# One sum moved to GpSimd at the entry of the attention layer, with the order of four engines rewritten around it

## The reference, cut to what matters

```
def sqrelu_mlp(h, w_up, w_down):
    return jnp.square(jax.nn.relu(h @ w_up)) @ w_down

for i in range(DEPTH):
    h = rmsnorm(x, g_mix_pre[i])
    m = conformer_conv(h, ...) if i % 2 == 0 else forgetting_attention(h, w_in, b_f, w_o)
    x = x + rmsnorm(m, g_mix_post[i])
    h = rmsnorm(x, g_ffn_pre[i])
    x = x + rmsnorm(sqrelu_mlp(h, w_up[i], w_down[i]), g_ffn_post[i])
```

## Time and profile before

| | |
|---|---|
| median of 3 runs | 1134.79 us (1134.19 to 1137.14) |
| the profiled execution, its own time | 1137.0 us |
| its span in the trace | 1135.3 us |
| PE busy | 1114.7 us (98%) |
| DVE busy | 933.9 us (82%) |
| ACT busy | 766.4 us (68%) |
| POOL busy | 292.0 us (26%) |

### The profile page before, as it was taken

One profiled execution on the slowest core, in us unless ns is written; L12 is line 12 of the kernel. 1 busy time (PEld: TensorE's weight loads), 2 busy tenths in 40 slices (PEclk: granted clock), 3 DMA queues, 4 the chain that ended last, 5 costly groups with the idle time before them and its releaser, 6 DMA issues. The chain is left out here.

```text
span 1135.3 us, 18229 instructions
## 1 busy us (share of the span) xinstructions
PE 1114.7 (98%) x6452; PEld 976.9 (86%) x6452; DVE 933.9 (82%) x1348; ACT 766.4 (68%) x1266; POOL 292.0 (26%) x269
## 2 busy tenths in 40 slices
PE   8999999999999999999999999999999999999997
PEld 7788888987898998998887888878888998988986
DVE  5899965679889689688798888894789889688688
ACT  6778878556785584675787777775566783674764
POOL 5688870221111020112421111100312020111014
PEclk9999989999999999999999999999999999999999
DMA  5322132275966676595222423232477777567673
GB/s 165 103 74 74 38 110 57 60 226 146 196 163 134 195 162 162 130 234 112 57 56 68 104 65 87 84 84 74 145 204 159 180 168 183 120 143 193 160 196 100
DMA packets 137268, 146.73 MB, mean 129 GB/s; under 512 B 5949, under 2 KB 108349, under 8 KB 136682
## 3 DMA queue, kind: packets, MB, share of 16 engines
q1 hardware_dynamic: 112300, 109.68, 30.8%
q0 software_dynamic: 24816, 35.92, 19.8%
q10 hardware_dynamic: 78, 0.16, 0.1%
HBM read 137.09 MB, written 6.29 MB: 126 GB/s over the span
## 5 line engine op out<-in xcount | busy, mean ns | idle before, releaser
L1542 ACT ACTIVATE whi<-mraw 128x1024 fp32r<-128x1024 f32 x212 | 221.5, 1056 | 149.1 <-PE psum L1236 94.5
L2218 DVE TENSOR_TENSOR wlo<-mraw,whi 128x1024 fp32r<-128x1024 f32 x212 | 256.9, 1223 | 68.5 <-ACT whi L1542 68.1
L1234 PE MATMUL psum<-whi,aop_hi 128*128 128x512 f32 x448 | 176.3, 394 | 1.4 <-ACT acc L1843 0.9
L1235 PE MATMUL psum<-wlo,aop_hi 128*128 128x512 f32 x448 | 174.6, 390 | 0.0
L1236 PE MATMUL psum<-whi,aop_lo 128*128 128x512 f32 x448 | 174.6, 390 | 0.0
L887 PE MATMUL psum<-hhi,whi 128*128 128x512 f32 x372 | 149.3, 401 | 0.8 <-DVE wlo L2207 0.5
L889 PE MATMUL psum<-hhi,wlo 128*128 128x512 f32 x372 | 145.5, 391 | 0.0
L888 PE MATMUL psum<-hlo,whi 128*128 128x512 f32 x372 | 145.3, 391 | 0.0
L1222 PE MATMUL psum<-hhi,wlo 128*128 128x256 f32 x384 | 108.8, 283 | 0.0
L1221 PE MATMUL psum<-xlo,whi 128*128 128x256 f32 x384 | 108.8, 283 | 0.0
L1220 PE MATMUL psum<-hhi,whi 128*128 128x256 f32 x384 | 108.7, 283 | 0.0
(11 more groups left out here) (320 smaller groups left out, 2839.8 us busy)
## 6 DMA issues: line engine op xcount, KB each, us to landing
mraw<-in_mlp_w_up SPq DMA_DIRECT2D x64, 512.0 KB, 7.0
mraw<-in_mlp_w_down SPq DMA_DIRECT2D x64, 512.0 KB, 5.3
mraw<-in_mlp_w_down POOLq DMA_DIRECT2D x40, 512.0 KB, 7.2
mraw<-in_mlp_w_up POOLq DMA_DIRECT2D x24, 512.0 KB, 7.5
wraw<-in_conv_pw_w SPq DMA_DIRECT2D x20, 512.0 KB, 4.5
wraw<-in_attn_w_in SPq DMA_DIRECT2D x16, 512.0 KB, 4.8
x_copy<-xT SPq DMA_DIRECT2D x2, 2048.0 KB, 7.4
xT<-x_copy SPq DMA_DIRECT2D x2, 2048.0 KB, 11.3
```

The costliest lines, as they stand in the source:

```text
L1234: pe.matmul(o, ah, wh, start=kt == 0 and (not kept or c == 0), stop=False)
L1235: pe.matmul(o, ah, wl, start=False, stop=False)
L1542: a.activation(split_unit(whi, e), raw_unit(l, c, e_), ACT.Copy).then_inc(s["m_hi"], 1)
L2218: d.tensor_tensor(split_unit(wlo, e), raw_unit(l, c, e_), split_unit(whi, e).bitcast(F32), ALU.subtract).then_inc(s["m_ready"], 1)
```

## The change

- The sum of slots 4 and 3 goes to slot 4 instead of slot 3, in both layers; `OUT_ACC` names slot 4 for that quarter. What it writes is no longer what the adding transfer (or `last_22`) reads.
- In layer 0 GpSimd makes this sum, with a 128x1024 add issued right behind the adding transfer. In layer 1 DVE still makes it, without the wait on `last_22`.
- GpSimd adds the first half's squares after its three small constants, no longer before them.
- PE turns blocks 0 to 3 of the first half one matmul triple earlier (n = 12 instead of 13), and blocks 4 and 5 at n = 14 instead of 15. Then each kb has gate, unit 0 and unit 1 together; unit 2's blocks 0 to 4 stand before kb = 6, its blocks 5 to 7 after kb = 7, and the second half's first two turnings follow kb = 6 and kb = 7.
- ACT makes the high part of unit 1 before the first `half_hi`, that of unit 2 after the first square, and the second half's sums of squares and root stand among `half_hi` 4 to 7; the squares 6 and 7 come after the second half's `by_token`.
- DVE splits unit 1's weights before `half_lo` 0, adds P4 at k = 3 and 4, splits unit 2's weights at k = 6, and inverts the second half's root before `half_lo` 7.

```
-OUT_ACC = ((3, 2), (1, 0))
+OUT_ACC = ((4, 2), (1, 0))
...
             g.dma_start(acc[:, ACC[P5], :, :], acc[:, ACC[P7], :, :],
                         accum_op=ALU.add).then_inc(v7_sum[0], 16)
-            add_half_squares(0)
+            g.tensor_tensor(flat(acc[:, ACC[P6], :, :]), flat(acc[:, ACC[P6], :, :]), flat(acc[:, ACC[P7], :, :]),
+                            ALU.add).then_inc(s["q_sum"], 1)
             pool.wait_ge(s["m_unit"], MLP_UNITS)
...
+            add_half_squares(0)
             add_half_squares(1)
...
-                if n == 13:
+                if n == 12:
...
-                if n == 15:
+                if n == 14:
...
-            pe.wait_ge(s["p_evac"], 5 * (CHUNKS - 1) + EVAC_NTH[P6])
-            for kb in range(2):
+            pe.wait_ge(s["p_evac"], 5 * CHUNKS)
+            for kb in range(KB):
+                if kb == 2:
+                    turned(0, 3)
+                if kb == 6:
+                    pe.wait_ge(w_ready[1], 2 * N_ATT + 2)
+                    for k in range(5):
+                        half_unit(2, 0, k)
                 pe.wait_ge(s["h1_ready"], kb + 1)
                 half_gate(0, kb)
-            pe.wait_ge(s["p_evac"], 5 * CHUNKS)
-            weights(N_ATT, 1)
-            for kb in range(KB):
-                if kb == 1:
-                    turned(0, 3)
-                if kb >= 2:
-                    pe.wait_ge(s["h1_ready"], kb + 1)
-                    half_gate(0, kb)
                 for u in range(2):
+                    if kb == 0:
+                        weights(N_ATT, u)
                     half_unit(u, 0, kb)
-            pe.wait_ge(w_ready[1], 2 * N_ATT + 2)
-            for kb in range(KB):
-                if kb == 4:
+                if kb >= 6:
                     pe.wait_ge(s["nrm_d"], 4)
-                    turned(1, 0)
-                    turned(1, 1)
+                    turned(1, kb - 6)
+            for kb in range(5, KB):
                 half_unit(2, 0, kb)
...
+            split_hi_att(1)
+            half_hi(0, 0)
+            half_hi(0, 1)
+            half_square(0, 0)
+            split_hi_att(2)
+            half_square(0, 1)
+            half_hi(0, 2)
+            half_square(0, 2)
+            half_hi(0, 3)
+            sum_squares(0, 0, 1)
+            half_hi(0, 4)
+            sum_squares(0, 1, 1)
+            half_square(0, 3)
...
             def last_21(l):
-                if l == 0:
-                    dve.wait_ge(v7_sum[0], 16 * (v_nth(0, CHUNKS - 1, "down") + 1))
-                else:
-                    dve.wait_ge(s["t22_done"], 1)
-                d.tensor_tensor(accs(P7), accs(P6), accs(P7), ALU.add).then_inc(s["q_sum"], 1)
+                dve.wait_ge(s["p_evac"], 5 * CHUNKS * (l + 1))
+                d.tensor_tensor(accs(P6), accs(P6), accs(P7), ALU.add).then_inc(s["q_sum"], 1)
...
             for k in range(KB + 1):
                 if k < KB:
                     x_half(0, k)
+                if k == 1:
+                    split_lo(N_ATT, 1)
+                if k == KB:
+                    token_inverse(0, 0)
                 if k:
                     half_lo(0, k - 1)
-                if k == 2:
-                    split_lo(N_ATT, 1)
+                if k in (3, 4):
+                    last_t2(0, k - 3)
                 if k == 6:
-                    last_21(0)
-            for tt in range(2):
-                last_t2(0, tt)
-            split_lo(N_ATT, 2, single=True)
-            token_total(0, 0)
-            token_inverse(0, 0)
+                    split_lo(N_ATT, 2, single=True)
+                    token_total(0, 0)
```

More of the change, by code:

```diff
@@ L2071, in _ @@
                 by_token(t, 1)
-            for k in range(KB):
-                half_hi(0, k)
-                if k == 1:
-                    split_hi_att(1)
-                if k:
-                    half_square(0, k - 1)
-                if k in (4, 5):
-                    sum_squares(0, k - 4, 1)
-                if k == 5:
-                    split_hi_att(2)
-            half_square(0, KB - 1)
-            for t in (0, 1):
-                sum_squares(0, t, 0)
+            split_hi_att(1)
[11 more added lines that the diff above has]
+            half_square(0, 3)
+            half_hi(0, 5)
+            sum_squares(0, 0, 0)
+            half_hi(0, 6)
+            sum_squares(0, 1, 0)
+            half_square(0, 4)
             token_root(0, 0)
+            half_hi(0, 7)
+            half_square(0, 5)
             act.wait_ge(s["tneg_done"], 2)
@@ L2088, in _ @@
                 by_token(t, 1)
+            for k in (6, 7):
+                half_square(0, k)
             for k in range(KB):
@@ L2882, in last_t2 @@
                 dve.wait_ge(s["q_sum"], 3 * l + 3)
-                o = acc[:, ACC[P7], tt, :]
+                o = acc[:, ACC[P6], tt, :]
                 d.tensor_tensor(o, o, psum[:, PBANK[P4] + tt, :], ALU.add).then_inc(s["comb"], 1)
```

## The result

The changed kernel takes 1139.45 us in the median of 19 runs, the kernel before 1135.41 us in 19 runs on the same chip. The ratio is 1.0028, with a 95% interval of 1.002 to 1.0037: slower by 3.2 us (0.0028 times 1135.4), where 0.6 us less was forecast. On the forecast's base this is 1134.79 times 1.0028 = 1138.0 us, above the range of 1132.5 to 1136.3. The profiled execution took 1138.41 us by its own time, its span is 1136.7 us, the mean granted clock of PE 0.995.

What follows compares the result with a forecast made beforehand. PE, busy 98% of the span, was taken to bound the kernel. The second half starting 0.52 us earlier plus 0.11 us at the end gave 0.63 us off 1134.79: 1134.2 us, range 1132.5 to 1136.3.

Steps and rivals of the forecast that it cites:

- the old stalls: First half: PE waits for DVE's low parts of units 1 and 2, 0.93 and 0.98 us, 1.91 us together.
- Steps 1 and 2: Entry: nothing changes up to unit 0's split; the earlier turning waits for nothing; alone, unit 1's split causes no PE stall.
- Steps 3 and 4: Entry: GpSimd's sum, ready 534.6, runs 535.94 to 538.34, delaying unit 1's split; PE stalls 1.39 us before the first gate matmul.
- The second rival: Entry: GpSimd's sum gets in ahead of unit 0's split, at 534.85; 0.2 us slower, 1135.0 us; chance 0.12.
- The second stall and its cover: At unit 2: its earlier split removes PE's 0.98 us stall, with about 0.8 us of cover.
- Port by the whole instruction: DVE and GpSimd share ports, locked for a whole instruction; DVE instructions with two SBUF inputs take part.
- Slot 3 read twice: Entry: the adding transfer reads slot 3 while GpSimd's sum does; costs nothing, or 1.6 us.
- the third rival: Entry: GpSimd's sum takes L812's whole 4.00 us, delaying unit 1's split; 1.0 us slower, 1135.8 us; chance 0.10.
- the fourth: After the entry: a later wait grows by what the entry gains; 1134.8 us; chance 0.12.
- The first rival: Entry: nothing holds up unit 1's split; both stalls go, 2.0 us gained, 1132.8 us; chance 0.16.
- The end of the program: Layer 1: DVE's sum no longer waits for `last_22` and starts 0.11 us earlier, all seen in the span.
- Given back downstream: First pair of heads or a weight transfer: a wait grows by the entry's gain; 1134.8 us; chance 0.12.

Runs made afterwards that it cites:

- Experiment 1: Changed kernel with the sum of slots 4 and 3 back on DVE in layer 0, at k = 3; ratio 1.0014 to the kernel before.
- Experiment 3: Changed kernel with GpSimd's sum waiting until DVE has scaled its two quarters; ratio 0.9993 to the kernel before.
- experiment 10: Changed kernel with PE's turnings one triple later again (n = 13 and 15); ratio 1.0003 to the kernel before.
- experiment 8: Changed kernel with 12 spare matmuls on PE in front of the first turning; ratio 1.0015 to the kernel before.
- experiment 5: Kernel of Experiment 1 with DVE's sum moved ahead of `half_lo` 2; ratio 0.9986 to the kernel before.
- experiment 6: Changed kernel, sum on DVE behind `half_lo` 2, P4 added at k = 4 and 5, ACT's `half_hi` 2 and 3 earlier; ratio 0.9988 to the kernel before.
- experiment 4: Changed kernel with GpSimd's sum cut into four adds of 128x256; ratio 1.0036 to the kernel before.
- experiment 7: Changed kernel with 24 spare matmuls on PE in front of the first turning; ratio 1.0028 to the kernel before.
- experiment 9: Changed kernel with GpSimd's sum waiting only for DVE's 128x2 negation; ratio 1.0022 to the kernel before.
- experiment 2: Kernel before with only the sum of slots 4 and 3 moved to GpSimd, old order kept; ratio 1.001 to the kernel before.

## Why the prediction was wrong

*What bounds the kernel, and the old stalls.* Right. Both stalls for weight blocks are gone. PE is busy 98% of the span in both. Without stalls the first half takes 14.28 less 1.19 = 13.09 us, forecast 13.34.

*Steps 1 and 2.* Their first sentence, "Up to unit 0's split nothing changes", is what fell. Experiment 1 shows that without GpSimd's sum they hold: turning at 1.69 us, first gate matmul at 5.08, 0.10 from where it stood, no stall ahead of it.

*Steps 3 and 4, the step that failed.* "The sum can begin at about 534.6" took the end of the transfer's recorded issue for the time from which GpSimd goes on, and "GpSimd gets its turn when unit 0's split is over" followed from it. The sum's record starts 0.62 us behind the issue's start, in the clock of before at 534.22. In the kernel before the negation stands there (533.94 to 534.20) and the scaling behind it. In the changed kernel the negation's record is open from 532.94 on, and it ends only behind GpSimd's sum; the scaling on DVE, the one on ACT, the turning and PE wait with it, 2.48 us where the prediction had no wait. The kernel before had a row that would have told it, GpSimd's next issue starting before the end of the one in front:

```profile
909.81 1.28 POOL L748 DMA_DIRECT2D mraw<-in_mlp_w_up  x1 [16.32 <-DVE wlo L2218]
910.57 1.76 POOL L756 DMA_DIRECT2D mraw<-in_mlp_w_down  x1
```

Experiment 3 shows it from the other side. There the sum comes behind the scaling, at 534.98 in the clock of before (step 3 had 534.6), and waits for unit 0's split. Its end, unit 1's split, PE's stall and the second half's start then come out within 0.2 us of step 4, and the ratio is the forecast's (0.9993; forecast 1134.2 over 1134.79 = 0.9995).

*The second rival* was the right mechanism: GpSimd in front. It was priced at +0.2 us instead of 3.2, for three reasons that the runs separate. It put GpSimd behind the scaling that PE's turning needs, while the sum caught the negation, so that the wait fell on PE inside the down product and not on a split with cover behind it. The change moved the turning one triple earlier, to where PE arrives at 1.69 us: nothing to wait for in the forecast, but 0.66 us more of standing (2.48 against 1.82, experiment 10). And it left out what a standing PE costs afterwards: 1.63 us at half clock (experiment 8; the sum above), and 1.19 us at blocks 3 and 4, where ACT's list, and by it DVE's, is tied to the last down matmul (next paragraph). The clock's part goes when the turning goes back (experiment 10) or PE is kept busy (experiment 8); the standing itself, 1.82 us and 0.87 us in experiment 10, goes only when GpSimd's sum does not stand ahead of the scaling (experiments 1, 3, 5 and 6).

*The second stall and its cover.* Right that it goes. "What would make all of this wrong is a PE stall at block 2 or at unit 2": it came at blocks 3 and 4. The prediction had "`half_hi` 2 ... ends at 540.1 + 0.40 + 0.49 = 541.0" and "PE wants block 2 ... at 542.5", a cover of 1.5 us. But 1.39 of it was the stall that PE was to have ahead of the first gate matmul, behind the same last down matmul that ACT waits for. Where PE does not stand there, the cover is not there either: the changed kernel and experiments 4, 7, 8 and 9 have 1.19 or 1.20 us at blocks 3 and 4. Where it does stand, the stalls nearly go: 0.34 us behind 0.87 in experiment 10, 0.29 behind 1.24 in experiment 3. The half clock is not the cause, since experiment 8 has none. Part may come from the P4 additions that DVE now makes between the low parts, and from ACT's high part of block 2 behind unit 2's split; experiment 6 relaxes both and has 0.37 us and less at each block. The size goes with PE's standing over all these runs, but none was made to separate the causes. I cost this at nothing; it is 1.19 us.

*Port by the whole instruction.* Right in kind. The Trainium skill, "SBUF — State Buffer", the part on the two sides of the memory, says that of the two engines the one that starts first gets the pair of ports for its whole instruction, and that VectorE's two-port modes, which a tensor_scalar can enter, take part as well as instructions with two SBUF inputs. I had read it for two-input instructions alone. The holding up of a 128x2 TENSOR_SCALAR for 2.98 us and of the scaling in experiment 9 agrees with the second half. With the first half the records do not agree as they stand: the negation's begins 0.28 us before GpSimd's (532.94 and 533.22), in experiment 4 0.29 before, and yet it is DVE that waits. Either GpSimd holds the ports earlier than its record begins or DVE later; no run tells these apart.

*Slot 3 read twice.* The sum took 2.67 us while the transfer read the same slot, 0.27 more than the subtraction of the same size in the earlier trace rows; whether the double reading or the other operation makes the 0.27, no run tells. The prediction names two rivals wrongly here: the 1.6 us for it are the third rival's size, not the fourth's, and the case in which the sum costs DVE nothing is the first, not the second. The first rival ("nothing holds up the split") and the third (a sum that runs its whole 4.00 us) did not come about: experiment 3's sum took 3.30 us, some 0.9 of it waiting for unit 0's split.

*The end of the program.* The 0.1 us is there from one sum to the next (1.64 instead of 1.74), but "The whole 0.11 us should be seen" was wrong: DVE's last addition waits for PE's last down matmul, and nothing of it is left in the span. It is worth 0.

*Given back downstream.* The kind of wait was right, its size and place only in part. The loss at the second half (+3.24) is still there at the scores (+3.57), so nothing is given back in the first pair of heads. But 1.2 us of it are gone at the end, 0.75 of them where ACT waited for a weight transfer. Of the 0.3 us at 807 us I have only that PE stood 0.15 us for a low part there in the kernel before and does not in the changed one. What also stays open is the 0.33 between second half and scores. In all kernels with the sum on GpSimd PE stands 1.11 or 1.12 us in front of the first scores, in the kernel before and in experiments 1, 5 and 6 it is 0.76 or 0.77. DVE's `gates_q` waits 0.5 instead of 0.2 us there, for ACT by the profile. The same kernels are those in which DVE has one instruction less (1347 against 1348), so the sum on GpSimd and the shorter list cannot be told apart. No run changed that place, and I have no cause for it.

## What to carry to other kernels

Before an instruction goes to GpSimd, find every DVE instruction that can meet it, tiny ones and those of one SBUF input included, and ask who waits for each: a negation of 256 numbers can pay for a whole 128x1024 add. Give the add an order against the critical short chain, by a semaphore (experiment 3: 4 us) or by leaving it on DVE in a gap that the trace shows (experiment 5), and do not cut it into pieces and hope. Price a stall of PE with what follows it, the matmuls at half clock and the engines whose lists are tied to PE's last matmul, and do not move a turning earlier where what it waits for is not early too. When a wait has cover, look whether the cover is itself a stall that the forecast counts on: it goes when the stall goes.

## What the runs showed of the hardware

- **GpSimd goes on before the recorded end of a transfer's issue.** The next instruction started 0.62 us after the start of an issue of 0.90 us in the changed kernel and in experiments 2 and 4, and 0.69 us after one of 0.98 us in experiment 9, where it waits for the negation.
- **Who gets the ports.** GpSimd got in between two back-to-back TENSOR_SCALAR of DVE (0.88 us became 3.26), and by the reading of L812's 4.00 us in the earlier trace rows did not between back-to-back differences of two SBUF operands. In experiment 3, where a split had begun 0.18 us before the sum, the sum took 3.30 us and ended 2.26 us behind the split's recorded end. DVE did not get in between four back-to-back adds of GpSimd (experiment 4). The sum itself took 2.67 to 2.69 us where it came first, against 2.40 in the earlier trace rows.
- **A DVE instruction held up ends where its own work puts it behind GpSimd's end**: 0.03 to 0.04 us for 128x2, 1.08 us for a split of 128x1024 (538.18 to 539.26), as 1.09 in the earlier trace rows.
- **PE's clock behind a stall.** Where PE had stood 2.48, 2.87, 2.05 and 2.09 us (the changed kernel, experiments 4, 9 and 1), the granted clock fell from 1.00 to 0.50, its lower level of 1.2 GHz, at the time that PE began again or up to 1.2 us later, for some 3 us; where it had stood 1.24 us (experiment 3) or 1.82 us (2 and 10) or been kept busy with spare matmuls (7 and 8), it stayed at 1.00. At the lower level the 512-column matmuls start 0.42 to 0.43 us apart instead of 0.22 to 0.23, the 256-column ones 0.21 instead of 0.12. In the changed kernel this came to 1.63 us on top of the stall.
- **Spare matmuls.** A 128-column float32 matmul with its weight load took 0.22 us (12 in 2.67 us, 24 in 5.36) and stands as two records.
